# The first stage of a two-layer decoder step: a split load of the constants, and another order of two norms, a projection and the gates

## The reference, cut to what matters

```python
up = rmsnorm(xp, norm_mix[i])
us = rmsnorm(xs, norm_mix[i])
mk, mv = mem_kv(mem_prompt, norm_mem[i], w_mem_kv[i])      # rmsnorm(mem, g) @ w: 256 memory rows
...
hp, qxp, st_p = mlstm_mixer(up @ w_in_a[li], ...)          # q, k, v, o, gates, memory queries
...
xp = xp + jnp.concatenate([hp, mem_attention(qxp, mk, mv)], axis=-1) @ w_out[i]
```

## Time and profile before

| what | value |
|---|---|
| device time, median of 3 runs | 2057.97 us (2050.64 to 2069.44) |
| span of the profiled execution | 2058.4 us |
| the profiled execution's own time, as far as shown | its span; no other time is given for it |
| TensorE matmul busy | 1896.0 us, 92% |
| VectorE busy | 1337.0 us, 65% |
| ScalarE busy | 931.9 us, 45% |
| DMA moved | 457.93 MB, mean 222 GB/s |

### The profile page before, as it was taken

How to read it: one execution, slowest core, us unless ns; L and a number is a source line. 1 busy time by engine, 2 the same in 40 slices (tenths; PEclk the granted TensorE clock), 3 DMA queues, 4 the chain that set the end, 5 groups by cost and what they waited for, 6 DMA issues and landing times.

```text
span 2058.4 us, 28180 instructions
## 1 busy us (share of the span) xinstructions
PE 1896.0 (92%) x10322; PEld 1522.1 (74%) x10322; DVE 1337.0 (65%) x1761; ACT 931.9 (45%) x1247; POOL 134.8 (7%) x180
## 2 busy tenths in 40 slices
PE   5999977999999999999877888999999999999994
PEld 3666646999874587777644777888888888888883
DVE  4362577787533366778543356888888888888884
ACT  0122120000011146666544215777777777777772
POOL 0000100010100000000000000111001110011001
PEclk8999888999999989999889688999999999999997
DMA  4422436476661333333489345999999999999992
GB/s 171 147 99 82 98 86 195 164 263 195 189 233 42 104 100 123 124 123 124 154 297 361 104 139 194 344 338 354 371 348 339 337 353 375 342 339 339 353 380 74
DMA packets 195812, 457.93 MB, mean 222 GB/s; under 512 B 12099, under 2 KB 77759, under 8 KB 194426
## 3 DMA queue, kind: packets, MB, share of 16 engines
q1 hardware_dynamic: 187970, 423.00, 58.3%
q0 software_dynamic: 7744, 33.65, 5.3%
HBM read 443.75 MB, written 21.32 MB: 226 GB/s over the span
## 4 chain that ended last, share of the span: by engine, by line
PE 73%; DVE 6%; issue 3%; DMA 2%; SPq 2%; ACT 1%; POOLq 0%; POOL 0%; DVEq 0%; ACTq 0%
PE bank L2420 67%; PE bank L2423 6%; SPq L2287 1%; DMA arena<-in_cache_nsa 1%; DVE arena L1563 1%; ACT arena L2970 1%; DVE uT L2687 0%; DMA arena<-in_cache_nsa_win 0%; DMA ring<-in_cache_nsa 0%; DMA ring<-scr_y,mem_all 0%; DVE rtmp L2680 0%; DVE arena L1721 0%; DMA scr_imp<-ring 0%; DVE small L1723 0%; DVE arena L1738 0%
## 5 line engine op out<-in xcount | busy, mean ns | idle before, releaser
L2420 PE MATMUL bank<-arena_r 128*128 128x448 f32 (+2 forms) x3296 | 813.6, 361 | 18.1 <-DVE uT_r L668 10.1
L2420 PEld LDWEIGHTS bank<-arena_r 128*128 128x128 f32 x3296 | 607.8, 189 | 94.4 <-issue 15.4
L1870 DVE TENSOR_TENSOR ring_r<-ring,arena_r 128x1792 fp32r<-128x1792 f32 (+1 forms) x216 | 443.4, 2087 | 48.0 <-ACT arena_r L2970 46.6
L2970 ACT ACTIVATE arena_r<-ring 128x1792 fp32r<-128x1792 f32 (+1 forms) x216 | 370.1, 1726 | 154.5 <-PE bank L2420 133.9
L2970 ACT ACTIVATE arena<-bank 64x256 f32<-64x256 f32 (+11 forms) x403 | 170.7, 434 | 401.0 <-PE bank L2420 234.5
L2420 PE MATMUL bank<-arena 128*128 128x256 f32 (+18 forms) x1506 | 253.1, 359 | 7.0 <-ACT arena L2970 5.2
L2420 PE MATMUL bank<-ring_r,arena_r 128*128 128x448 f32 (+1 forms) x840 | 246.1, 374 | 0.0
L2420 PEld LDWEIGHTS bank<-arena 128*128 128x128 f32 (+10 forms) x1506 | 172.8, 172 | 63.6 <-issue 38.4
L2420 PEld LDWEIGHTS bank<-ring_r,arena_r 128*128 128x128 f32 x840 | 157.7, 188 | 21.6
L1870 DVE TENSOR_TENSOR arena_r<-arena,arena_r 128x1792 fp32r<-128x1792 f32 (+1 forms) x72 | 138.4, 1935 | 52.4 <-ACT arena_r L2970 51.1
L2423 PE MATMUL bank<-consts_sb,arena 128*128 128x128 f32 (+6 forms) x736 | 118.9, 291 | 35.6 <-DMA arena<-in_x_sample 10.3
(11 more groups left out here) (385 smaller groups left out, 1760.4 us busy)
## 6 DMA issues: line engine op xcount, KB each, us to landing
ring<-in_w_moe_gu SPq DMA_DIRECT2D x144, 896.0 KB, 6.9
ring<-in_w_moe_d SPq DMA_DIRECT2D x60, 1024.0 KB, 6.0
ring<-in_cache_nsa SPq DMA_DIRECT2D x176, 256.0 KB, 4.5
arena<-in_w_moe_gu SPq DMA_DIRECT2D x48, 896.0 KB, 6.2
ring<-in_w_ffn_gu SPq DMA_DIRECT2D x22, 1024.0 KB, 7.3
arena<-in_cache_nsa SPq DMA_DIRECT2D x80, 256.0 KB, 6.2
ring<-in_w_in_a SPq DMA_DIRECT2D x8, 1536.0 KB, 7.3
arena<-in_w_moe_d SPq DMA_DIRECT2D x12, 1024.0 KB, 6.3
```

Of the source, the lines that this page charges most:

```text
L1870: V.tensor_tensor(unit_low(c), unit_slot(c), unit_high(c), ALU.subtract).then_inc(S("m_sp"), 1)
L2420: return nc.tensor.matmul(out, lhsT, rhs, start=first, stop=last, **kw_)
L2970: return nc.scalar.activation(out, in_, fn, **kw_)
```

## The change

The load of the constants is split: identity and ones come first, the rest after the small rows, and it counts into `ld_rows`. In the ring, `gxa` comes ahead of `mkv0`. The eight pieces of the memory rows are now copied by ScalarE, which also squares each piece from the bank into `mem_sq` (the place of `mem_u_a`); the three small copies go to ScalarE too. The tokens' norm is norm 0, and the matmuls with ones over the memory squares follow it, in bank 0. The memory rows are multiplied by root and gain after `uT` is written. TensorE projects gates and memory queries, then memory keys and values (banks 0 and 1), then starts the loop over slices; the keys are transposed after slice 1. On VectorE the gates' chain comes ahead of the copies of keys and values, and `log_forget` on ScalarE ahead of the loop.

```diff
-            sp.dma_start(consts[:, :], I["consts"]).then_inc(S("ld_const"), 16)
+            first = CONSTS["ones"][0] + CONSTS["ones"][1]
+            sp.dma_start(consts[:, 0:first], I["consts"][:, 0:first]).then_inc(S("ld_const"), 16)
...
+            sp.dma_start(consts[:, first:], I["consts"][:, first:]).then_inc(S("ld_rows"), 16)
...
+    std("gxa", ("g_mm", 3), wa, 3072, 3344)
     std("mkv0", ("mkv_mm", 2), wm[0], 0, 512)
-    std("gxa", ("g_mm", 3), wa, 3072, 3344)
...
-                m = mm(bank[5 + i][:, :], mem_u[:, k, P * i:P * i + P], w[:, k, :], k == 0, k == KT - 1)
+                m = mm(bank[5 * L + i][:, :], mem_u[:, k, P * i:P * i + P], w[:, k, :], k == 0, k == KT - 1)
...
-                pe.wait_ge(*done("set_ev", k + 5))
+                pe.wait_ge(*(done("set_ev", k + 5) if k < 4 else done("mt_ev", k - 3)))
...
-            pe.wait_ge(S("ld_rows"), 96)
+            pe.wait_ge(S("ld_rows"), 112)
...
-            norm(0, NMEM)
-            norm(1, NT)
-            pe.wait_ge(S("mem_u"), 1)
-            w = got("mkv0")
-            mem_project(mm, w, 0, 0)
-            mem_project(mm, w, 0, 1)
-            mem_turn(pe, tr, 0)
-
-            pe.wait_ge(S("nrm_out"), 2)
-
+            norm(0, NT)
+            pe.wait_ge(*done("mt_ev", KT))
+            for k in range(KT):
+                m = mm(bank[0][:, 0:NMEM], ones, mem_sq[:, k, :], k == 0, k == KT - 1)
+            m.then_inc(S("nrm_mm"), 1)
+
+            pe.wait_ge(S("nrm_out"), 1)
             w = got("gxa")
-            pe.wait_ge(S("mkv_ev"), 3)
+            pe.wait_ge(*done("mt_ev", 9))
...
+            pe.wait_ge(S("mem_u"), 1)
+            w = got("mkv0")
+            mem_project(mm, w, 0, 0)
+            mem_project(mm, w, 0, 1)
...
-            pe.wait_ge(S("g_ev"), 2)
...
                 if t >= 2:
                     pe.wait_ge(*done("qk_ev", t - 1))
+                else:
+                    pe.wait_ge(S("mkv_ev"), t + 1)
...
+                if t == 1:
+                    pe.wait_ge(S("g_ev"), 2)
+                    mem_turn(pe, tr, 0)
...
-            for k in range(KT):
-                dve.wait_ge(*done("set_mm", KT + k + 1))
-                link(V.tensor_copy(memT[:, k, :], bank[k % 4][:, 0:NMEM]), "set_ev")
...
-            norm(0, memT[:, :, :], NMEM, memT[:, :, :], None)
+            norm(0, xT[:, :, :], NT, uT[:, :, :], MIX0)
+            dve.wait_ge(S("nrm_mm"), 2)
+            link(V.tensor_scalar(rtmp[:, 0:NMEM], bank[0][:, 0:NMEM], 1.0 / D, EPS, ALU.mult, ALU.add))
+            link(V.reciprocal(rtmp[:, 0:NMEM], rtmp[:, 0:NMEM]), "nrm_rc")
+            dve.wait_ge(S("nrm_rs"), 2)
+            link(V.tensor_tensor(memT[:, :, :], memT[:, :, :], bc(rstd[:, 0:NMEM], 1, KT), ALU.mult), "nrm_out")
             link(V.tensor_tensor(mem_u_a, memT[:, :, :], bc(gain[:, MEM0 * KT:MEM0 * KT + KT], 2, NMEM), ALU.mult), "mem_u")
-            norm(1, xT[:, :, :], NT, uT[:, :, :], MIX0)
-            mem_rows_dve(dve, link, V, 0)
-            mem_turn_dve(dve, link, V, 0)
-            link(V.memset(preP[:, :, 0:3], 0.0), "pre0")
...
             link(V.tensor_tensor(gs[:, 10, :], a_, mts, ALU.subtract), "mt_s")
+            mem_rows_dve(dve, link, V, 0)
+            link(V.memset(preP[:, :, 0:3], 0.0), "pre0")
+            mem_turn_dve(dve, link, V, 0)
...
-            root(0, NMEM)
-            root(1, NT)
-            act.wait_ge(*done("pre0"))
+            for k in range(KT):
+                act.wait_ge(*done("set_mm", KT + k + 1))
+                link(f(memT[:, k, :], bank[k % 4][:, 0:NMEM], ACT.Copy))
+                link(f(mem_sq[:, k, :], bank[k % 4][:, 0:NMEM], ACT.Square), "mt_ev")
+            act.wait_ge(*done("set_mm", 17))
+            link(f(gain[:, :], bank[4][:, 0:56], ACT.Copy))
+            link(f(cw, bank[4][0:MD, 64:128], ACT.Copy))
+            link(f(hg, bank[4][0:MD, 128:136], ACT.Copy), "mt_ev")
+            root(0, NT)
+            root(1, NMEM)
...
             beside = memory_act(act, link, f, 0)
+            log_forget()
+            act.wait_ge(*done("pre0"))
             for t in range(16):
-                if t == 2:
-                    log_forget()
```

More of the change, by code:

```diff
@@ L53 @@
     "proj_ev": (("woa_ev", 8), ("bq_ev", 6), ("bkv_ev", 9), ("wob_ev", 8)),
-    "turn_ev": (("set_ev", 17), ("cvo_ev", 4), ("kn_ev", 2), ("kd_ev", 8), ("om_ev", 6), ("ur_lo", 6)),
+    "turn_ev": (("set_ev", 8), ("cvo_ev", 4), ("kn_ev", 2), ("kd_ev", 8), ("om_ev", 6), ("ur_lo", 6)),
     "once_dve": tuple((n, 1) for n in (
-        "pre0", "mt_s", "ms_q0", "ms_d0", "bd0", "ms_p0", "ms_pte0", "mixm0", "bT_ev", "vsw", "qk_done", "n_s", "bd", "hsq0", "hsq", "den", "u_split0",
+        "mt_s", "pre0", "ms_q0", "ms_d0", "bd0", "ms_p0", "ms_pte0", "mixm0", "bT_ev", "vsw", "qk_done", "n_s", "bd", "hsq0", "hsq", "den", "u_split0",
         "bg_ev", "ms_q1", "q12", "ms_d1", "qr_ev", "ms_p1", "ms_pte1", "mixm1", "pc_d0", "pc_w", "pc_oe", "pz0", "pc_d", "pc_p", "imp", "sel", "pc_d1", "pc_p1", "imp1", "sel1",
@@ L59 @@
         "m_ex", "f_acc0", "f_acc1", "f_rc0", "f_y0", "f_rc1", "f_y1", "f_acc2", "f_rc2", "f_y2")),
-    "copied": (("qk_ev", 16), ("v_ev", 6), ("o_ev", 8)),
+    "copied": (("mt_ev", 9), ("qk_ev", 16), ("v_ev", 6), ("o_ev", 8)),
     "unit_mm": (("ff_mm", 30), ("m_pe", 288)),
@@ L393, in build @@
         mem_u_a = area(P, KT, NMEM)
+        mem_sq = mem_u_a
         def halves(*places):
@@ L690, in mem_rows_dve @@
                 dve.wait_ge(S("mkv_mm"), 2 * L + i + 1)
-                link(V.tensor_copy(mkv[:, i, :], bank[5 + i][:, :]), "mkv_ev")
+                link(V.tensor_copy(mkv[:, i, :], bank[5 * L + i][:, :]), "mkv_ev")
         def mem_turn_dve(dve, link, V, L):
@@ L2425, in norm @@
             def norm(n, width):
-                pe.wait_ge(S("nrm_sq"), n + 1)
+                pe.wait_ge(S("nrm_sq"), max(n, 1))
                 for k in range(KT):
@@ L2682, in norm @@
                 r = rstd[:, 0:width]
-                if g is None:
-                    link(V.tensor_tensor(dst, src, bc(r, 1, KT), ALU.mult), "nrm_out")
-                    return
                 for k in range(KT):
```

## The result

| | median | runs |
|---|---|---|
| before | 2059.01 us | 4 (2050.64 to 2069.44) |
| changed | 2032.48 us | 4 (2030.57 to 2035.86) |

The ratio is 0.986, 95% interval 0.9831 to 0.989: faster by 1.1 to 1.7%. The medians lie 26.5 us apart. In two more sessions the same kernel gave 0.9838 (0.9805 to 0.9872) and 0.9864 (0.984 to 0.9889), with medians 30.2 us (2060.44 and 2030.28) and 30.6 us (2063.19 and 2032.60) apart. The profiled execution's own time was 2030.57 us with a span of 2028.8: 1.8 us lie around the span, where I had put nothing.

The account below looks back on a forecast made before the run. TensorE, busy 92% of the span, was taken as the bound, so only idle, slow-clock and start time could be gained: 15.5 + 5.2 = 20.7 us, then 2058.4 - 20.7 - 0.4 = 2037.3, stated as 2037.5; range 2028 to 2047.

Parts of the forecast that it names:

- The load: Before TensorE's first transposition: splitting the constants' load starts TensorE at 6.5 us, 3.8 earlier; bounds 3.3 to 3.9.
- Set-up and norm: First transposition to `uT`: ScalarE's pieces 0.82 us each, tokens' norm starts at 18.2, takes 6.1, `uT` ready at 31.9.
- rival (c): Set-up: no extra table load, norm 0 in 3.7 us, no slow gates: 2032.3; chance 0.62 together with the forecast.
- The new hole: Ahead of the gates: TensorE waits 4 us for `uT`; slow clock behind it costs 0 to 2.9 us, taken as 1.5.
- Projection and keys: Gates to slice 2: projection ends at 62.1, VectorE's copies covered by 3 us, slice 2 at 70.0, 15.5 us earlier.
- Rival (a): Loop over slices: VectorE late all the same, TensorE waits at slice 7 as before; 15.5 us gained, 2042.9; chance 0.08.
- The hole at 107.9: Loop over slices: VectorE catches up by slice 4, removing a 3.7 us wait and 1.5 of slow clock: 5.2 us.
- The sum: Whole kernel: 15.5 + 5.2 = 20.7 us, gained early and reaching the end whole; forecast 2037.5.
- a sign of being wrong: After 345 us: the prediction is wrong if the lines there have not moved by the same amount.
- the fast set-up: Set-up: no extra load (+1.3), norm 0 in 3.7 us (+2.4), no slow gates (+1.5): 2032.3; chance 0.62 with the forecast.
- The switch of tables: Between the norm's reciprocal and root: one extra table load, bounds 0 and 1.28 us, taken as 1.28; skill page says 2.66.

Follow-up runs that it names:

- the kernel with the hole filled: Changed kernel plus 8 extra matmuls, output unread, in TensorE's 4.2 us hole between memory sum and gates; Silu mark at 164.7 us.
- its own experiment: Changed kernel with memory pieces, their squares and the small copies back on VectorE; Silu mark at 164.6 us.
- the kernel with the logs early: Kernel before with only ScalarE's Exp and Ln of the gates moved ahead of slice 0 instead of slice 2; Silu mark at 182.2 us.

## Why the prediction was right, point by point

The forecast was 2037.5, the median 2032.5; the gain was 26.5 by medians against 20.7. The mechanism held up to the Silu mark, with errors of a few tenths to 1 us that partly cancel. Behind the mark it did not: the gain was not just carried on.

*The load.* 3.8 us forecast, 3.3 to 3.4 measured: TensorE began at 6.9 to 7.3 against 10.3 to 10.5. That is the lower bound that I had set. The reckoning mixed two units: its 2130 KB count 1000 bytes to the KB and its 1457 KB count 1024, so it should have read 4.0 us, not 3.9, which widens the miss to 0.6 or 0.7. `gxa` landed at 16.5 (16) and `mkv0` at 21.8 (22), as reckoned.

*Set-up and norm.* ScalarE's pieces were 0.83 us apart (forecast 0.82), the norm started at 18.69 (18.2) and took 5.3 (6.1). `uT` was ready at 31.5 (31.9), with the table load that I had taken at its upper bound. In the second profile of the changed kernel the same matmuls took 3.9 us, near the 3.7 of rival (c), the clock up early. Whether it was the clock isn't shown. Here are 3 us of the norm in the first and the second profile of the changed kernel, and in the kernel with the hole filled:

```profile
19.00:22.00 3.00, 3.00 (x9) 2.32 (x9) 0.00 (x0) 2.27 (x8) 2.92 (x6) 1.00 1.05 383
```

```profile
19.00:22.00 3.00, 3.00 (x15) 2.58 (x14) 0.00 (x0) 2.60 (x9) 2.97 (x6) 1.00 1.04 382
```

```profile
19.00:22.00 3.00, 3.00 (x9) 2.32 (x9) 0.00 (x0) 2.72 (x9) 2.88 (x6) 0.55 1.05 383
```

The first profile ran at the pace of the third line, whose clock was 0.55, yet its own granted clock reads 1.00. So a slow clock is likely, but the rows don't say it, and the words "slow clock" of the expectations for this norm go further than the trace.

*The new hole.* 4.2 us (4), and the slow clock behind it cost 1.7 (1.5), read from the gates' 32 records at either clock.

*Projection and keys.* The loop began at 61.6 (62.1), slice 2 at 69.2 (70.0), which is 16.3 us earlier than before (15.5). TensorE never waited for the copies of keys and values; the cover was 2.7 us (61.62 less the end of the first copy, 58.95) against 3 reckoned. Rival (a) did not occur: at slice 4, as reckoned, VectorE waited for ScalarE's copy (1.18 us at 80.67) and no longer lagged. Of the 16.3 us some 3.4 are the load. The other 13, from the order of the norms and of what follows, no experiment took out alone: they are read from the timelines, where the holes of 3.5 and 9.9 us are gone and one of 4.2 has come. ScalarE's help is next to nothing in them, as its own experiment showed.

*The hole at 107.9.* 5.2 us forecast, 5.4 to 6.3 by the kernel with the logs early: 5.4 against the first and second profile of before, 6.3 against the third. In the first pair it was 21.8 - 16.3 = 5.5.

*The sum.* 20.7 forecast at the Silu mark, 21.8 in the first pair of profiles, 23.3 between the means of three (189.0 and 165.7). What was off in size is the claim that this gain reaches the end whole. The prediction named a sign of being wrong: that the lines after 345 us have not moved by the same amount. They had not. In the first pair they lie 25.6 us apart from 371 to 846 us and 29.5 to 30.0 from 1205 us on. The sign itself was too strict, since the kernel before alone does the same: its second profile was 2.8 us behind the first at the mark and 0.7 ahead at 371 us. That the result came out better than the forecast, by 5 us, owes most to this part, which the sum had at nothing, and which the rows put down mostly to the clock of unchanged stages. That it stayed inside the range, whose lower end was made of the fast set-up and of scatter, was luck as far as this part goes. I had counted run-to-run scatter as symmetric about one profile of before, but the executions of before ran from 2050.6 to 2069.4, and its median moved to 2063.2 in the last session. The prediction also took the span for the whole time; 1.8 us lie around it. Within 1% or faster was a coin's throw by my sum; the measured interval, 1.1 to 1.7%, is on the faster side, and nothing in the forecast had chosen that side.

*The switch of tables.* What the Trainium skill (ScalarE: Activation LUTs, Table sets) says of cheap functions in every set agrees with the load that appeared once a copy came first, and vanished with a root first. The drain that the same page of the Trainium skill counts into its 2.66 us (section What ACT_TABLE_LOAD costs) does not show: without the load the root came 0.1 us behind the reciprocal, with it 1.37.

## What to carry to other kernels

Order the start by who is the last to be ready: load what the first transposition reads ahead of everything else, and put the operand of the long matmul chain ahead of side work. Look at where a late engine comes from: a wait of 3.7 us at slice 7 came from two logs that were queued two slices too late, 20 us earlier. A helper on another engine can bring its own price: its first activation decides which table is in place when the root is due. Judge terms of a few microseconds by marks at the same instruction in several profiles, since the whole time of the kernel before ranged over 19 us on its own (2050.6 to 2069.5) and even the marks over 2.8.

## What the runs showed that I had not expected

The same instructions take several times: 8.76 or 7.07 us for 32 gate records and 222.8 or 230.7 us from 576 to 799 us, with the granted clock lower in the longer one each time, and 3.9 to 6.75 us for the 16 records of the tokens' norm, where in the changed kernel the clock's rows don't tell the two apart. Behind holes of the same 2.9 us the clock was down in one kernel and up in another. This moved profiles of the kernel before by up to 11.3 us behind the mark, 7.9 of it in one stretch in which TensorE waited no longer than otherwise.
